# Low parts of the first feed-forward's weights, formed by GpSimd between its slab loads instead of by VectorE

## What is computed

```python
h2 = rmsnorm(x, norm2_g)                                  # 512 x 1024
x = x + jnp.square(jax.nn.relu(h2 @ w_up)) @ w_down       # w_up 1024 x 4096, w_down 4096 x 1024
...
mod_l = (jax.nn.silu(c) @ w_mod + b_mod)                  # w_mod 1024 x 6144, one row c
mod_c = (jax.nn.silu(c_ctx) @ w_mod + b_mod)
```

## Time and profile before

| | |
|---|---|
| time, median of 3 runs | 1949.51 us (1945.78 to 1952.19) |
| the profiled execution's own time | 1948.73 us |
| its span, first to last instruction | 1947.0 us |
| TensorE busy, share of the span | 1826.4 us, 94% |
| VectorE busy | 1124.1 us, 58% |
| ScalarE busy | 694.9 us, 36% |
| GpSimd busy | 460.0 us, 24% |
| mean granted TensorE clock | 0.965 |

### The profile page before, as it was taken

The page is one execution under the profiler, slowest core; times in us unless marked ns, Lnnn a source line. Parts: engine busy times, 40 slices in busy tenths (PEclk is TensorE's granted clock), DMA queues, the critical chain, the costliest instruction groups (busy, mean ns, idle before and its releaser), DMA issues.

```text
span 1947.0 us, 20621 instructions
## 1 busy us (share of the span) xinstructions
PE 1826.4 (94%) x7251; PEld 1249.0 (64%) x7251; DVE 1124.1 (58%) x2133; ACT 694.9 (36%) x1131; POOL 460.0 (24%) x443
## 2 busy tenths in 40 slices
PE   7997898999997999999999989999998799999997
PEld 3546632368875878887845455656565378888885
DVE  5968443244447755676423155656574487777776
ACT  3253445433344321232142134535360343323224
POOL 2732200020012100010000113131321156656552
PEclk9997798999998999999999999999998899999999
DMA  5263200043332544454302112111110324232411
GB/s 138 70 124 106 76 1 0 17 119 92 103 124 87 180 145 150 162 181 143 119 1 79 51 44 55 43 43 41 37 55 22 97 65 130 82 113 65 130 44 44
DMA packets 184811, 164.42 MB, mean 84 GB/s; under 512 B 17559, under 2 KB 168787, under 8 KB 184715
## 3 DMA queue, kind: packets, MB, share of 16 engines
q1 hardware_dynamic: 172363, 123.99, 21.4%
q0 software_dynamic: 11808, 39.29, 6.8%
q10 hardware_dynamic: 560, 0.12, 0.0%
HBM read 153.73 MB, written 4.21 MB: 81 GB/s over the span
## 4 chain that ended last, share of the span: by engine, by line
PE 78%; DVE 11%; issue 4%; ACT 3%; DMA 1%; POOL 1%; POOLq 0%; ACTq 0%; DVEq 0%; SPq 0%
PE bank L1403 27%; PE bank L1746 18%; PE bank L1509 10%; PE bank L1521 4%; PE bank L1342 2%; DVE arena L2467 2%; PE bank L1196 2%; PE bank L1356 2%; PE bank L1626 2%; PE bank L1298 1%; PE bank L1634 1%; PE bank L1548 1%; PE bank L1585 1%; DVE arena L3192 1%; PE bank L1099 1%
## 5 line engine op out<-in xcount | busy, mean ns | idle before, releaser
L3328 DVE SCALAR_TENSOR_TENSOR arena<-bank,ffn_taps,arena 128x441 f32<-128x441 f32 (+2 forms) x352 | 220.3, 687 | 86.9 <-ACT arena L2427 86.9
L1509 PE MATMUL bank<-hT,ring 128*128 128x512 f32 x448 | 198.4, 597 | 0.0
L2837 DVE TENSOR_TENSOR w_lo<-ring,w_hi 128x2048 fp32r<-128x2048 f32 x52 | 119.2, 2292 | 126.3 <-ACT w_hi L2031 122.2
L1403 PE MATMUL bank<-h_lo,w_hi 128*128 128x512 f32 x448 | 178.3, 398 | 6.1 <-issue 4.8
L2031 ACT CAST w_hi<-ring 128x2048 fp32r<-128x2048 f32 x52 | 98.8, 1900 | 190.6 <-PE bank L1403 190.6
L1403 PE MATMUL bank<-hT_hi,w_hi 128*128 128x512 f32 x384 | 156.5, 408 | 4.7 <-DVE h_lo L2923 4.7
L1055 POOL TENSOR_TENSOR w_lo<-ring,w_hi 128x2048 fp32r<-128x2048 f32 x22 | 104.6, 4755 | 186.0 <-ACT w_hi L2401 121.8
L1509 PEld LDWEIGHTS bank<-hT,ring 128*128 128x128 f32 x448 | 84.4, 192 | 98.0 <-issue 97.8
L1403 PE MATMUL bank<-act_hi,w_hi 128*128 128x512 f32 x352 | 139.2, 396 | 4.7 <-DVE act_lo L2965 4.7
L1746 PE MATMUL bank<-hT_hi,w_hi 128*128 128x512 f32 x336 | 133.2, 396 | 0.3 <-POOL w_lo L1055 0.3
L1746 PE MATMUL bank<-hT_hi,w_lo 128*128 128x512 f32 x336 | 133.0, 396 | 0.0
(11 more groups left out here) (491 smaller groups left out, 3587.3 us busy)
## 6 DMA issues: line engine op xcount, KB each, us to landing
ring<-in_w_up SPq DMA_DIRECT2D x76, 512.0 KB, 4.8
arena<-in_w_mod POOLq DMA_DIRECT2D x48, 512.0 KB, 4.2
ring<-in_w_in SPq DMA_DIRECT2D x72, 256.0 KB, 3.3
ring<-in_w_down SPq DMA_DIRECT2D x32, 512.0 KB, 3.9
ring<-in_w_in SPq DMA_DIRECT2D x30, 512.0 KB, 4.0
arena<-in_w_down SPq DMA_DIRECT2D x22, 512.0 KB, 4.2
ring<-in_w_out SPq DMA_DIRECT2D x8, 512.0 KB, 3.9
ring<-in_w_out SPq DMA_DIRECT2D x16, 256.0 KB, 2.9
```

The costliest lines, as they stand in the source:

```text
L1403: ins = pe.matmul(out, u[:, n % SLOTS, cols], v[:, k, :], start=start and k == w[0][0] and m == 0, stop=stop and k == w[-1][0] and m == 2)
L1509: ins = pe.matmul(o, w[:, k, :], src[:, k, 0:n], start=k == 0, stop=k == DT - 1)
L2837: ve.tensor_tensor(w_lo[:, n % SLOTS, :], ring[:, n % SLOTS, :], value(w_hi[:, n % SLOTS, :]), ALU.subtract)\
L3328: return ve.scalar_tensor_tensor(o[:, ys, xs], x[:, yt, xt], ffn_taps[:, at:at + 1], o[:, ys, xs], ALU.mult, ALU.add)
```

## The change

GpSimd gets a helper `low` of its own. Behind the two DMA issues of slab n = 12h + r it forms, for r < 8, the low part of chunk r+2 of the half (counted over the up chunks and on into the down chunks); for r = 8 to 11 it forms the low parts of the down chunks 2r-14 and 2r-13, as far as the half has them (in half 0 the last two are chunks 0 and 1 of `up1_1`). VectorE's calls of `low` in both stages go, 16 in half 0 and 14 in half 1. Nothing else changes: the low parts of the first two chunks of `up1_0` stay with VectorE.

```diff
+            def low(name, c):
+
+                n = C0[name] + c
+                pool.wait_ge(hi_ready, SPLIT0[name] + c + 1)
+                pool.tensor_tensor(w_lo[:, n % SLOTS, :], ring[:, n % SLOTS, :], value(w_hi[:, n % SLOTS, :]), ALU.subtract)\
+                    .then_inc(split_ready, 1)
...
                     pool.dma_start(mod_w[:, half], src.rearrange("(k p) n -> p k n", p=P)).then_inc(mod_in[half], 16)
+                h, r = divmod(n, 12)
+                if r < 8:
+                    low(f"up1_{h}", r + 2)
+                else:
+                    for m in range(2 * r - 14, 2 * r - 12):
+                        if m < (10, 8)[h]:
+                            low(f"down1_{h}", m)
...
                                          value(act_hi[:, ds(4 * i + k, 1), :]), ALU.subtract).then_inc(act_ready, 1)
-                        if k % 2:
-                            low(n + 2 + k // 2, q + 2 + k // 2, 2 * i)
...
-                def round_(i, splits):
+                def round_(i):
                     step.enter(i, 28)
                     for m in range(2):
                         for k in range(2 * m, 2 * m + 2):
                             weigh(6 * h + 4, k, 0, i)
                         for k in range(2 * m, 2 * m + 2):
-                            if k + 2 < splits:
-                                low(n + 2 + k, q + 2 + k, 4 * i)
-                        for k in range(2 * m, 2 * m + 2):
                             full(ve, t + k, 4 * i)
```

More of the change, by code:

```diff
@@ L2983, in round_ @@
                             out_of(t + k, ve.tensor_tensor(x, acc[(t + k) % BANKS][:].unsqueeze(1), x, ALU.add))
[L2985 to L2995, removed]
+                with ve.Fori(0, 2) as i:
+                    round_(i)
+                step.leave(2)
                 if h == 0:
```

## The result

The changed kernel takes 2059.60 us (median of 4 runs, 2056.65 to 2059.93); the kernel before, run beside it, takes 1947.64 us (4 runs, 1940.49 to 1952.19). The ratio is 1.0574, with an interval of 1.0550 to 1.0598: slower by 5.7%, some 112 us. The prediction was 2054 us, with a range from 2003 to 2076. The profiled execution took 2059.33 us, and its span is 110.6 us longer than that of before.

What follows compares the result with a forecast made beforehand. The prediction took the up-stage stretch to be bound by TensorE, with 0.7 us slack for slabs. Up half 0 48.9, up half 1 53.5 and down stages 2.5 made 104.9 us on 1948.73: 2054 us, range 2003 to 2076.

Steps and rivals of the forecast that it cites:

- The likeliest case: Up stages: loads behind GpSimd's subtraction come late, VectorE is held off, every second chunk waits; 2054 us, chance 0.63.
- From a chunk's end to the late `take`: Up stages: subtraction, slab issue, landing and VectorE's weighing put the `take` 23.1 us after a chunk's end, TensorE idle 11.4.
- The holding off: Up stages: GpSimd's subtraction and VectorE's two-SBUF-operand instructions exclude each other for a whole instruction; pair costs 13.65 us, by sharing 11.15.
- Every second chunk waits: Up stages: of every two chunks one waits for its slab, and the pair costs 13.65 us more.
- Rival A: Up stages: no holding off and quick landings, a pair costs 8.35 us; 61 us in all, 2010 us, chance 0.22.
- Rival B: Up stages: VectorE was the bound and slabs come in time; only -2.5 us at slab 0, 1946 us, chance 0.04.
- gain of 2.5 us at slab 0: Start of up half 0: GpSimd's eight multiplications move behind VectorE's first `weigh`, so its wait is 2.5 us shorter.
- Rival C: More held up: stretched subtraction, landings of 5.5 us, down slabs all late by 1 us; 2067 to 2074 us, chance 0.11.
- Down stages: Down stages: between 0 and 1 us late at five slabs (9 to 11, 21 and 22), half taken, 2.5 us.
- Up half 1: Up stage of half 1: slab 12's `take` late, 12.5 us with slow start, then three pairs, 41.0; together 53.5 us.
- Up half 0: Up stage of half 0: 11.2 us behind after chunk 2, two pairs 27.3, last wait 10.4; together 48.9 us.
- the 2.2 us: TensorE behind a long wait: 48 matmuls take 13.50 us rather than 11.31 at the slow clock, another 2.2 us.

Runs made afterwards that it cites:

- experiment 2: The changed kernel with GpSimd's subtraction replaced by three memsets of about the same length that read nothing: 2021.31 us, ratio 1.0392 to the kernel before.
- experiment 1: The kernel before, VectorE still subtracting, with GpSimd only waiting behind each slab's load for the low part it would have formed: 2005.47 us, ratio 1.0310.
- experiment 3: The changed kernel with each GpSimd subtraction issued one slab later, so a slab's loads go out ahead of it: 1951.72 us, ratio 1.0032 to the kernel before.
- experiment 4: The kernel of experiment 3 with GpSimd's subtraction replaced by three memsets that read nothing: 1947.00 us, ratio 0.9990 to the kernel before.
- experiment 7: The kernel before with GpSimd's eight multiplications moved from ahead of slab 1's load to ahead of slab 9's: 1941.62 us, ratio 0.9959.
- experiment 8: The kernel of experiment 7 with each down stage begun after 8 of 16 activation tiles: 1933.39 us, ratio 0.9926 to the kernel before.

## Why the prediction was right, and where its sizes were off

The likeliest case was the one that came, and its chain holds step by step. The feed-forward became 112.3 us longer, forecast 104.9.

- *From a chunk's end to the late `take`*: +23.1 forecast, +23.3 here. The subtraction took its 4.6 us and the issue followed at once; the landing, 5.0 in the forecast, was 5.2 to 5.6 at six of the eight slabs (4.2 at slab 1, 8.0 at slab 12). `weigh` half 0 stands as reckoned.
- *The holding off*: forecast was a subtraction from +15.6 to +20.2, with the product ahead of it and `act_lo` behind it; at slab 3 it ran from 665.00 to 669.71, which is +15.0 to +19.7. There it was the product that was held, not `act_lo` (the landing was later than reckoned), and the end was the same to 0.5 us. At slabs 5, 7 and 12 it was `act_lo`, as forecast. In the forecast's words one holds the other off for a whole instruction: experiment 2 shows it, since it is gone with the reading. The Trainium skill (SBUF — State Buffer, Who interferes with whom) names exactly this condition, two SBUF inputs on VectorE against a GpSimd instruction that reads, and not one that only writes; the 4.98 us beside the subtraction and 0.68 us beside the memset agree with it.
- *Every second chunk waits*: right, and for the 10 to 12 us foretold (10.9 to 11.8). The sum had eight such slabs and the trace has the same eight; the forecast's last paragraph says "some 7", which was a miscount of its own sum.
- *Rival A* (no holding off, quick landings, 2010 us) is, but for its landings (5.8 us in the median, not 4.2 to 5.0), what experiment 2 built: 2021 us. It failed because the holding off is there. The sign that it named, a wait of 2 to 4 us at every chunk, was no sign of it: experiment 2 has no holding off and waits at every second one. *Rival B* (VectorE was the bound, 1946 us) fell: its gain of 2.5 us at slab 0 came, and that was all. VectorE was through at 610.9, not 612.0, in a stage that began 1.5 us later, so 2.6 us earlier in its place, and TensorE's wait there fell from 5.2 to 2.6 us. The forecast put this gain down to four rows of `weigh`, which would give only 1.5 us; the rest came from the product, `act_lo` and the rows ahead of them, stretched likewise before. *Rival C* came in part: landings of 5.5 us and down slabs that all miss.

What was off:

- **Down stages, 2.5 us forecast, 7.5 measured.** This is the term that was mis-sized. I had given each of five slabs between 0 and 1 us and taken half. TensorE waits 1.2 to 1.6 us at each instead, 7.1 in all. VectorE's timeline and the chain of the changed kernel there:

```profile
785.49 0.62 DVE L2962 TENSOR_SCALAR rstd<-arena,silu_c 128x256 f32<-128x256 f32 x2 [11.98 <-DMA arena<-in_w_mod]
786.02 10.36 DVE L2964 SCALAR_TENSOR_TENSOR rstd<-arena,silu_c,rstd 128x256 f32<-128x256 f32 x14
```
```profile
796.53 1.05 PE bank L1446 x8
...
821.10 1.05 PE bank L1446 x8
...
845.64 1.05 PE bank L1446 x8
```

The 14 rows that took 6.00 us take 10.36, nearly the whole subtraction more, as reckoned. In experiment 2, without the holding off, no such slab is late. But the landing there was 5.1 to 5.5 us where I had put 4.65, and at slab 9 the cast began 0.4 us later in the stage. The `take` itself, 1.05 us for 0.79, adds to each. Waits and `take`s make 8.4 us; the 7.5 is less by luck, because the first 96 matmuls of the second down stage took 22.03 us and not 23.43, while those of the first took 24.07 and not 23.71. Where two ends lie 1 us apart on a path without slack, the middle was no better founded than the end.

- **Up half 1, 53.5 forecast, 57.0 measured.** The first `take` came 22.25 us after the stage's start, forecast 22.1, although the second half of that slab landed 8.0 us after its issue, not 5.0: it landed while `act_lo` was held off (4.64 us long), and so cost nothing. What was left out is the `take` behind a wait, which takes 1.01 us and not 0.34 (0.60 at slab 12): 2.4 us more at the four waits. The earlier trace rows has it at 612.16, and I counted only the matmuls behind it. The matmuls took 13.47 to 14.02 us, forecast 13.50, and the three later `take`s came 23.1 to 23.3 us behind the chunk's end, forecast 23.1; that is the rest.
- **Up half 0, 48.9 forecast, 47.8 measured.** The same `take`s, 0.67 us longer at four waits, were more than made up for: the first late `take` came 45.6 us after the stage's start, forecast 46.4, and the matmuls behind the next ones took 12.66, 12.96 and 13.40 us rather than 13.50. These are stretches of 5 us behind the wait, TensorE alone, in the changed kernel: us, busy (x matmuls), granted clock, DMA share, GB/s.

```profile
637.38:642.40 5.02, 5.02 (x17) 0.72 0.53 178
674.30:679.30 5.00, 5.00 (x15) 0.65 0.65 214
710.84:715.84 5.00, 5.00 (x13) 0.55 0.77 257
869.95:874.95 5.00, 5.00 (x12) 0.50 0.85 286
999.93:1004.93 5.00, 5.00 (x22) 1.00 0.00 0
```

The clock was at the lower level, 0.50, for all of these 5 us only at the first two waits of half 1 (0.53 and 0.54 at the next two); in half 0 it came back within them, behind waits of the same 11 us. So the 2.2 us that the forecast took from one row was an upper value for half 0 and right for half 1. The last line is the second down stage's start: behind a wait of 2.4 us the clock had not fallen at all, where before it read 0.71 at the same place behind the same wait. The length of the wait alone does not say what the clock does behind it.

That the loss is the place and the holding off together, some 76 (with the subtraction's length) and 36 us of 112, is shown by experiments 1 to 4. That several transfers released at one moment make the landing longer (median 4.2 us before, 5.5 after) is only argued; nothing was run that keeps the order and spreads the loads.

## What to carry to other kernels

Before work is put on an engine that issues loads, ask which load stands behind it and what the work waits for: here a subtraction of 4.6 us behind a wait for another engine put each prefetch 8 us into the very chunk at whose end it was wanted, and 106 of the 112 us came back by issuing the same loads one step earlier. A low busy share (24%) did not say that GpSimd had room, and the 69 us taken off VectorE were worth almost nothing, since TensorE waited for it only 5.7 us at the `take`s and 4.7 us ahead of the down stages. Where the two share SBUF, reckon with the whole length of GpSimd's instruction at each meeting, and ask whether that meeting falls on slack.

## What the runs showed that I had not expected

- A VectorE instruction with a single tensor operand of SBUF was held off too: the `TENSOR_SCALAR` over 128 x 256 took 4.60 us beside GpSimd's subtraction, 0.35 us elsewhere (experiment 3). I had reckoned with the two-input ones alone.
- The slab's landing went from a median of 4.2 us to 5.5 us in the changed kernel. In experiment 1, where GpSimd forms no low part, it was 6.7, and 9.0 at most; in experiment 7, whose loads go out as before, 4.3. So it needs no arithmetic on GpSimd. But experiments 3 and 4, whose loads stand in the same order, had 4.9 and 5.5, so the order alone does not set it either.
- After stalls of about 11 us TensorE's granted clock over the next 5 us lay anywhere between 0.50 and 0.72 in the same kernel, and after one of 2.4 us it stayed at 1.00. So the slow clock that experiment 8 took away behind the down stages' starts (23.71 us for 96 matmuls, now 21.90) is not a fixed price of such a wait: the changed kernel had the wait at its second down stage without it.
